# Second norm, merge, tail and the order of an expert step in a hybrid decoder step

## The reference

```python
z = x @ w_in                                  # RWKV, windowed attention, memory attention, 3 gates
o_a, o_b, o_m = rwkv(z), window_attention(z), memory_attention(z)
g = sigmoid(gates)                            # three blocks of 1024
merged = g[0] * (o_a @ p_a) + g[1] * (o_b @ p_b) + g[2] * (o_m @ p_m)
x = LayerNorm(ALPHA * x + merged @ w_o) * ln1_g + ln1_b
# top 1 of 4 groups, top 2 of its 8 experts, blocks of rows per expert
for e in range(32):
    y[e] = (silu(rows[e] @ e_gate[e]) * (rows[e] @ e_up[e])) @ e_down[e]
x = LayerNorm(ALPHA * x + sum_k gate_k * y_k) * ln2_g + ln2_b
```

## Time and profile before

| what | value |
|---|---|
| median of 3 runs | 1317.51 us (1314.8 to 1317.7) |
| the profiled execution | 1323.6 us, of which 1321.8 us lie between its first and its last instruction |
| TensorE busy, mean granted clock | 86%, 0.958 |
| VectorE, ScalarE, GpSimd busy | 33%, 18%, 7% |
| HBM read and written | 277.11 MB, 24.23 MB |
| expert loads (page, DMA issues) | 32 gate, 32 up, 2048 KB each, 36.9 us from issue to landing |
| DMA of GpSimd's queue | 5184 packets, 8.54 MB |

### The profile page before, as it was taken

The page is one execution under the profiler, slowest core; times in us unless marked ns, Lnnn a source line. Parts: engine busy times, 40 slices in busy tenths (PEclk is TensorE's granted clock), DMA queues, the critical chain, the costliest instruction groups (busy, mean ns, idle before and its releaser), DMA issues.

```text
span 1321.8 us, 21992 instructions
## 1 busy us (share of the span) xinstructions
PE 1133.8 (86%) x9315; PEld 792.9 (60%) x9315; DVE 432.0 (33%) x824; ACT 238.1 (18%) x413; POOL 98.7 (7%) x92
## 2 busy tenths in 40 slices
PE   7999989999899999999899944999877777777775
PEld 4888866777678888877774533455444444444432
DVE  5200003576555676524342245111111111111116
ACT  4000011234621111121110110121111111111102
POOL 0400000000000000000001100111111111111110
PEclk9999998899999999999999955999999999999998
DMA  9342242312221101242638064999999999999974
GB/s 332 124 137 64 79 143 63 89 49 72 56 53 56 50 27 46 64 157 75 244 110 336 32 282 178 387 420 425 421 422 425 422 423 424 424 423 422 423 295 194
DMA packets 53346, 293.04 MB, mean 222 GB/s; under 512 B 9995, under 2 KB 12109, under 8 KB 41738
## 3 DMA queue, kind: packets, MB, share of 16 engines
q1 hardware_dynamic: 48098, 283.55, 55.3%
q0 software_dynamic: 5184, 8.54, 1.7%
HBM read 277.11 MB, written 24.23 MB: 228 GB/s over the span
## 4 chain that ended last, share of the span: by engine, by line
PE 60%; DMA 25%; DVE 5%; SPq 4%; ACT 2%; issue 2%; DVEq 1%; POOL 0%; POOLq 0%; ACTq 0%
PE psum L717 57%; DMA arena<-in_e_down 19%; DVE arena L1536 3%; SPq L673 3%; PE psum L722 3%; DMA arena<-in_e_up 3%; ACT arena L1291 1%; DMA arena<-scratch_x,arena 1%; DMA arena<-in_p_abm 1%; DVE arena L1539 1%; DVEq L1571 0%; DMA arena<-in_w_mem_kv 0%; DMA arena<-in_w_in 0%; DMA arena<-scratch_ya 0%; SPq L661 0%
## 5 line engine op out<-in xcount | busy, mean ns | idle before, releaser
L717 PE MATMUL psum<-arena 64*64 64x64 f32 (+9 forms) x8808 | 1068.4, 337 | 151.9 <-DMA arena<-in_e_gate 31.8
L717 PEld LDWEIGHTS psum<-arena 64*64 64x64 f32 (+3 forms) x8808 | 738.5, 152 | 459.4 <-issue 218.8
L1291 ACT ACTIVATE arena<-psum 128x512 f32<-128x512 f32 (+11 forms) x144 | 88.1, 635 | 657.1 <-PE psum L717 393.6
L1536 DVE TENSOR_TENSOR arena<-arena,psum 128x256 f32<-128x256 f32 (+3 forms) x136 | 74.6, 548 | 342.5 <-PE psum L717 202.7
L1536 DVE TENSOR_TENSOR arena<-arena 128x1024 f32<-128x1024 f32 (+16 forms) x173 | 133.7, 784 | 33.5 <-PE psum L717 8.7
L722 PE MATMUL psum<-arena 128*128 128x128 f32 (+5 forms) x507 | 74.8, 281 | 22.1 <-DMA arena<-scratch_x,arena 8.1
L722 PEld LDWEIGHTS psum<-arena 128*128 128x128 f32 (+5 forms) x507 | 54.8, 145 | 54.6 <-issue 32.1
L1536 DVE TENSOR_TENSOR arena<-psum,arena 128x256 f32<-128x256 f32 (+4 forms) x85 | 47.0, 564 | 68.6 <-PE psum L717 64.4
L2186 POOL TENSOR_TENSOR arena<-arena 128x1024 f32<-128x1024 f32 (+1 forms) x10 | 27.2, 2733 | 469.0 <-DVE arena L1536 469.0
L2127 DVE COPY arena<-arena 128x1 uint32 (+1 forms) x32 | 4.9, 154 | 153.9 <-PE psum L717 153.9
L2231 POOL DMA_INDIRECT arena<-scratch_x,arena x32 | 32.7, 1023 | 283.0 <-DVE arena L2118 242.0
(11 more groups left out here) (114 smaller groups left out, 200.1 us busy)
## 6 DMA issues: line engine op xcount, KB each, us to landing
arena<-in_e_gate SPq DMA_DIRECT2D x32, 2048.0 KB, 36.9
arena<-in_e_up SPq DMA_DIRECT2D x32, 2048.0 KB, 36.9
arena<-in_e_down SPq DMA_DIRECT2D x21, 2048.0 KB, 36.8
arena<-in_w_in SPq DMA_DIRECT2D x46, 512.0 KB, 3.9
arena<-in_e_down SPq DMA_DIRECT2D x44, 512.0 KB, 34.4
scratch_gates<-arena SPq DMA_DIRECT2D x24, 260.0 KB, 4.1
arena<-scratch_gates SPq DMA_DIRECT2D x8, 780.0 KB, 4.5
arena<-in_p_abm SPq DMA_DIRECT2D x8, 640.0 KB, 5.7
```

Source lines behind the costliest of these rows:

```text
L717: return pe.matmul(out, a, b, start=start, stop=stop)
L1291: return act.activation(out, a, ACT.Copy)
L1536: return v.tensor_tensor(out, a, b, op)
```

## The change

- Merge: the window and memory projections of block 1 move from ahead of the group norm's spreading to behind branch 0 of block 0, and VectorE's products with them.
- Second norm: the transposes take the scaled row, ahead of gain and bias (`turn_normed`), and gain and bias come in at the eviction as a scalar per partition from a new tile `lnT` (one more small load on SyncE's queue), half of the channels on ScalarE, half on VectorE. The transposes of a tile stand between the halves of the next tile's `w_o` product, the logits behind it. Gain and bias of the rows themselves are both VectorE's, GpSimd's `offset(x1, 1)` is gone.
- Routing: the comparison rounds become a rounding by addition and subtraction of 1.5 * 2^23.
- Expert stage: down(e-1) stands ahead of up(e), on TensorE and in SyncE's queue. The last down matrix comes in two loads, and its product waits for each half apart.
- Tail: no lag; each tile is finished on VectorE with two passes of 1024 (subtract the mean and multiply by the gain; multiply by the reciprocal and add the bias); ScalarE makes only the root. GpSimd reads its register ahead of the last scatter's wait.

```diff
+HALF_DOWN = 0.5 / SB - 0.5
+WHOLE = 1.5 * 2.0 ** 23
...
@@ SyncE @@
             sp.dma_start(gb[:, 1, :], I["ln1_b"].partition_broadcast(P)).then_inc(s["out_in"], 16)
+            sp.dma_start(lnT, I["ln1_T"]).then_inc(s["out_in"], 16)
...
                     gate_load(e, (j - 1) % 3, e - 3)
+                    down_load(e - 1, (j - 2) % 3, e - 4)
                     up_load(e, j % 3)
-                    down_load(e - 1, (j - 2) % 3, e - 4)
-            down_load(NE - 1, (NE - 2) % 3, NE - 4)
+            sp.wait_ge(s["y_mm"], NE - 1)
+            sp.dma_start(ed[0][:, 0:2, :], wd[NE - 1][:, 0:2, :]).then_inc(s["ew0d_in"], 16)
+            sp.dma_start(ed[0][:, 2:4, :], wd[NE - 1][:, 2:4, :]).then_inc(s["out_in"], 16)
...
@@ TensorE @@
             gate_tile(G_MERGE + 1, (G_MERGE + 1) % 2, (G_MERGE + 1) // 2, 6)
-            pe.wait_ge(s["mgw1_in"], 32)
-            for g in (1, 2):
-                pe.wait_ge(s["proj_used"], g)
-                project(1, g, 2 * (g - 1))
...
-            pe.wait_ge(s["proj_used"], 3)
+            pe.wait_ge(s["proj_used"], 1)
             gate_tile(G_MERGE + 2, (G_MERGE + 2) % 2, (G_MERGE + 2) // 2, 0)
             pe.wait_ge(s["oa_ready"], 1)
-            for q in range(2):
-                project(q, 0, 4 + 2 * q)
+            project(0, 0, 4)
+            pe.wait_ge(s["mgw1_in"], 32)
+            pe.wait_ge(s["proj_used"], 2)
+            project(1, 1, 2)
+            pe.wait_ge(s["gate_out"], G_MERGE + 3)
+            project(1, 2, 0)
+            project(1, 0, 6)
...
+            def turn_normed(step):
+                u = tile_at(1, step)
+                n = rows(u)
+                pe.wait_ge(s["ln_scaled"], step + 1)
+                if step:
+                    pe.wait_ge(s["x1T_ready"], 2 * step)
+                for c in range(KD):
+                    last = turn(bank(4, KD, P)[:, c, 0:n], x1[0:n, u, c::KD])
+                last.then_inc(s["x1_turned"], 1)
...
+            for step in range(1, Q):
+                t = tile_at(1, step)
+                if step >= 2:
+                    pe.wait_ge(s["h_used"], step - 1)
+                for h in range(2):
                     for c in range(KD):
-                        last = turn(bank(4, KD, P)[:, c, 0:n], x1[0:n, u, c::KD])
-                    last.then_inc(s["x1_turned"], 1)
-                if step >= 2:
-                    logits(step - 2)
+                        last = mm(bank(2 * (step % 2) + h, 512), MG[:, c, t * P:t * P + P], wo[h][:, c, :], c == 0, c == KD - 1)
+                    if h == 0:
+                        turn_normed(step - 1)
+                last.then_inc(s["h_made"], 1)
+                logits(step - 1)
+            turn_normed(Q - 1)
             logits(Q - 1).then_inc(s["logits_made"], 1)
...
                 for k in range(FF // P):
+                    if half_in and k == 2:
+                        pe.wait_ge(s["out_in"], half_in)
...
                 turn_h_step(e - 1)
+                down_step(e - 1, d % 3, i * 2 + d // 3)
                 up_step(u % 3, i * 2 + u // 3)
                 if not last:
                     rows_step(e + 1, (j + 1) % 2, i * 3 + (j + 1) // 2)
-                down_step(e - 1, d % 3, i * 2 + d // 3)
...
-            down_step(NE - 1, (NE - 2) % 3, (NE - 2) // 3)
+            down_step(NE - 1, 0, (NE - 2) // 3, 112)
...
@@ ScalarE @@
-                copy(x1T[:, :, t * P:t * P + n], bank(4, KD, P)[:, :, 0:n]).then_inc(s["x1T_ready"], 1)
-
-            layer_norm(x1, 1, 0, before=lambda t: x1_turned(t - 1) if t >= 1 else None)
-            x1_turned(Q - 1)
+                for c in range(KD // 2, KD):
+                    last = act.activation(x1T[:, c, t * P:t * P + n], bank(4, KD, P)[:, c, 0:n], ACT.Identity,
+                                          bias=lnT[:, 1, c:c + 1], scale=lnT[:, 0, c:c + 1])
+                last.then_inc(s["x1T_ready"], 1)
+
+            act.wait_ge(s["out_in"], 96)
+            layer_norm(x1, 1, 0, after=x1_turned)
...
-            layer_norm(x1, 2, 1, tail=True)
+            for u in range(Q):
+                t = tile_at(2, u)
+                n = rows(t)
+                act.wait_ge(s["ln_stats"], 2 * Q + u + 1)
+                act.activation(rstd[0:n, t, :], mv[0:n, t, 1:2], ACT.Sqrt, bias=eps[0:n, 0:1]).then_inc(s["ln_std"], 1)
...
@@ VectorE @@
-            attention_branches(1)
...
+            v.wait_ge(s["gate_sig"], 2)
+            for n, (g, b) in enumerate(((1, 2), (2, 0), (0, 6))):
+                v.wait_ge(s["proj_made"], 4 + n)
+                gated(1, 1, g, b, n == 0)
+            v.sem_inc(s["merged"], 1)
...
-                        tt(x[0:n, i, :], x[0:n, i, :], gb[0:n, 0, :], ALU.mult).then_inc(s["ln_gained"], 1)
-                        if tail:
-                            v.drain()
-                            tt(x[0:n, i, :], x[0:n, i, :], gb[0:n, 1, :], ALU.add).then_inc(s["x_normed"], 1)
+                        if turned:
+                            turned(i, u)
+                        tt(x[0:n, i, :], x[0:n, i, :], gb[0:n, 0, :], ALU.mult)
+                        v.drain()
+                        tt(x[0:n, i, :], x[0:n, i, :], gb[0:n, 1, :], ALU.add).then_inc(s["x_normed"], 1)
...
-            ts(qb, rank, float(SB), ALU.is_ge)
-            ts(nx, cnt, float(SB), ALU.is_gt)
-            v.drain()
-            for q in range(2, N // SB + 1):
-                stt(qb, rank, float(SB * q), qb, ALU.is_ge, ALU.add)
-                stt(nx, cnt, float(SB * q), nx, ALU.is_gt, ALU.add)
-                v.drain()
+            ts(qb, rank, 1.0 / SB, ALU.mult, HALF_DOWN, ALU.add)
+            ts(nx, cnt, 1.0 / SB, ALU.mult, HALF_DOWN - 1.0 / SB, ALU.add)
+            v.drain()
+            ts(qb, qb, WHOLE, ALU.add)
+            ts(nx, nx, WHOLE, ALU.add)
+            v.drain()
+            ts(qb, qb, WHOLE, ALU.subtract)
+            ts(nx, nx, WHOLE, ALU.subtract, 0.0, ALU.max)
+            v.drain()
...
-            layer_norm(x1, 2, expert_sum, 1, tail=True)
+            for u in range(Q):
+                t = tile_at(2, u)
+                n = rows(t)
+                expert_sum(t, u)
+                src = bank(2 * t, D) if t < NT else x1[0:B, NT, :]
+                for h in range(2):
+                    v.bn_stats(st6[0:n, t, h, :], src[:, h * 512:(h + 1) * 512])
+                v.drain()
+                v.bn_aggr(mv[0:n, t, :], st6[0:n, t, :, :]).then_inc(s["ln_stats"], 1)
+                v.drain()
+                stt(x1[0:n, t, :], src, mv[0:n, t, 0:1], gb[0:n, 0, :], ALU.subtract, ALU.mult)
+                v.wait_ge(s["ln_std"], 2 * Q + u + 1)
+                v.reciprocal(rstd[0:n, t, :], rstd[0:n, t, :])
+                v.drain()
+                stt(x1[0:n, t, :], x1[0:n, t, :], rstd[0:n, t, :], gb[0:n, 1, :], ALU.mult, ALU.add).then_inc(s["x_normed"], 1)
...
@@ GpSimd @@
-            offset(x1, 1)
...
             scatter(NE - 2, 0)
+            n_extra = extra_count(g)
             scatter(NE - 1, 1)
```

More of the change, by code:

```diff
@@ L431, in tile_at, with extra_count, extra_blocks @@
             return (t - 1) % Q if pas else t
[L433 to L435 removed]
+        def extra_count(eng):
+            return eng.value_load(ovfi.bitcast(I32)[0:1, XB:XB + 1], min_val=0, max_val=XB)
+        def extra_blocks(eng, body, n=None):
+            n = extra_count(eng) if n is None else n
             with eng.If(n > 0):
@@ new lines, in turn_normed @@
+            def turn_normed(step):
[7 more added lines that the diff above has]
+                last.then_inc(s["x1_turned"], 1)
+            pe.wait_ge(s["gate_out"], N_GATE)
+            for c in range(KD):
+                for h in range(2):
+                    last = mm(bank(0, 512)[h * 64:h * 64 + B, :], MG[:, c, T:N], wo[h][:, c, :], c == 0, c == KD - 1)
@@ L1293, in _, with layer_norm @@
             eps = const("eps")
-            def layer_norm(x, pas, lag, before=None, after=None, tail=False):
+            def layer_norm(x, pas, lag, before=None, after=None):
                 scaled = s["x_scaled" if pas == 0 else "ln_scaled"]
@@ L1307, in layer_norm @@
                         act.wait_ge(s["ln_rs"], pas * Q + u + 1)
-                        src = bank(2 * i, D) if tail and i < NT else x[0:n, i, :]
+                        src = x[0:n, i, :]
                         act.activation(x[0:n, i, :], src, ACT.Identity, bias=nmr[0:n, i, :],
@@ L1544, in ts, with layer_norm @@
                 return v.tensor_scalar(out, a, s1, s2, op0, op1)
-            def layer_norm(x, pas, before, lag, tail=False):
+            def layer_norm(x, pas, before, lag, turned=None):
                 for t in range(Q + 2 * lag):
@@ L1967, in residual, with x1_turned @@
                 v.drain()
-            layer_norm(x1, 1, residual, 0)
+            def x1_turned(t, at):
+                n = rows(t)
+                v.wait_ge(s["x1_turned"], at + 1)
+                for c in range(KD // 2):
```

(5 more changed lines are left out.)

68 lines of the change are left out of this document (23 added, 45 removed).

## The result

| what | before | after |
|---|---|---|
| median | 1317.7 us (9 runs) | 1309.3 us (9 runs, 1304.6 to 1312.9) |
| ratio, 95% interval | | 0.9934 [0.9915, 0.9953], so 8.7 us less, between 6.2 and 11.2 |
| profiled execution: span | 1321.8 us | 1307.1 us |

The profiled executions differ by 14.7 us, more than the medians, since 5.1 of these lie ahead of the merge, in code that the change leaves alone: the eviction of the gate tile that the merge waits for stands at 605.73 before and at 600.65 after. The clock differs by as much: up to that eviction TensorE lost 17.1 us to the lower level in the one execution and 12.0 in the other. The sections on the experiments and on the hardware tell more of such differences. From here on only lengths of stretches are compared, each from an event that both kernels have.

What follows compares the result with a forecast made beforehand. The prediction took the DMA engines to bound the expert stage, with chains of waits before and behind it. Its terms, 5.7 + 2.45 + 2.44 - 2.0 - 0.45 + 0.5 + 3.2 = 11.8, took 1317.5 to 1305.7 us, range 1300 to 1311.

Steps and rivals of the forecast that it cites:

- Merge: Merge: waits for loads of 4.26 and 0.48 us and 1.7 of clock go, 0.75 is added; gain 5.7, bounds 3.0 to 7.2.
- Second norm: Last tile's chain: 3.70 and 1.6 us saved, 2.85 added ahead; gain 2.45, bounds 1.5 to 5.0.
- Routing: Routing on VectorE: three of eight pairs of comparisons are left; five fewer save 2.44 us.
- Expert stage: Expert stage, DMA-bound: the new order costs 2.0 us in the first steps and 0.45 at the end.
- Tail: Scatter to reload gains 0.5 us; third norm gains 3.2, the sample tile's passes moving into waits, 4.3 per prompt tile.
- The later third pair: First expert steps: up(1)'s load goes out 4.6 us later and the DMA engines run dry, losing 2.2 to 3.7 us.
- the old dip: First expert steps: the DMA share's dip to 0.78 at 848 to 852 us goes, giving back 0.9 us.
- The term for GpSimd's read: Scatter to reload: the register read is done earlier, under the last scatter's wait; gain 0.5 us, bounds 0 and 1.1.
- The first: Rival, expert stage: short idles bring cold spells and TensorE becomes the bound; about 1361 us, slower; chance 3%.
- one of the prediction's own signs of being wrong: Expert stage: a granted clock below 1.00 in its middle would show the prediction wrong.
- The second: Rival: DMA engines run dry longer in the expert stage (-4.6) and merge gives only 3.0; 1311 us; chance 17%.
- The third: Rival: clock stays up through the shorter waits of norm and spreading, +2.6 and +1.5; 1301.6 us; chance 15%.

Runs made afterwards that it cites:

- after_again: The kernel after, unchanged, run once more for a second trace: 99.1 us from the first w_o product to the scan.
- tail_only: The kernel before with only the third norm's change and GpSimd's early read: 29.6 us from the first product of the residual to VectorE's end.

## Why the prediction was right, and where it was not

The time, 1309.3, lies in the range and 3.6 us above the forecast of 1305.7. Part of that is luck: second norm and routing gave 2.4 us less than forecast and the merge 1.1 less, but the expert stage took 1.6 less than forecast. By stretches, means over all traces that have the old or the new form:

| stretch | old | new | gained | forecast |
|---|---|---|---|---|
| merge: gate tile's eviction to first w_o product | 86.9 | 82.3 | 4.6 | 5.7 |
| second norm and routing: to the scan | 101.2 | 98.7 | 2.5 | 4.9 |
| scan to the issue of eu2 | 20.7 | 20.7 | 0 | 0 |
| expert stage: to the first product of the residual | 469.9 | 470.7 | -0.9 | -2.45 |
| tail: to VectorE's end | 33.6 | 30.2 | 3.4 | 3.7 |
| sum | | | 9.6 | 11.8 |

**Second norm, the step that failed.** In the first pair of traces the norm itself took 85.2 us before and 85.9 after, and routing the rest: the term came out at -0.7 instead of +2.45. The prediction worked out the last tile's chain, and that came as it said. It set the first tile's at nothing and did not follow ScalarE's side of it: two waits ahead of a first square root, a table load behind the later one, and transposes moved to where they need the result. 1.43 us of wait and 1.7 of clock are the 3.1 missing. In the four traces with the early table load the term is 2.1 to 2.8, 2.4 on the mean, which is the forecast. The Trainium skill, "ScalarE: Activation LUTs", section on what ACT_TABLE_LOAD costs, measures about 1283 ns for the load and 1380 for a drain; the row agrees on the load (1.28), and the drain does not show. It does not show either where the load stands straight between an eviction and the next function (in the trace of after the eviction ends at 601.25, the load stands at 601.27 to 602.55, the function follows at 602.56).

**Merge.** The removed wait, its hiding and the new 0.79 were right. Mis-sized was what the clock gives back: 1.7 was taken for the spell behind the wait, with the other one kept at 1.5. The spell behind the spreading is not a constant: where it lost 1.7 the stretch gained just 5.7 (86.9 - 81.2), where 3.4, about 4.0. Why it is 1.7 in one execution and 3.4 or 5.1 in another is not shown.

**Routing.** 2.9 us (16.0 before, 13.1 after, from the last logits to the scan) against 2.44: the three rounds left have one tensor operand and take 0.24 per 128x160 instruction where those removed took 0.33, which makes it 2.7 by the rounds (3.91 - 1.23). The other 0.24 lies ahead of them, where VectorE had stood 0.46 us in the trace of before and does not in that of after; that is not explained.

**Expert stage.** The later third pair (4.9 us, 4.6 worked out) and a dip were right, and the dip is smaller: shares 0.85 and 0.82 over 8 us, 1.3 us, not 2.2 to 3.7. In its first window TensorE is busy 4.00 of 4.00 us: there the loads wait for TensorE. That the old dip goes in return rested on the earlier trace rows, and that was one execution's. At the end of the stage 0.9 of the stream's loss of 1.4 is left. The prediction let the end cost 0.45 more; in the first trace of after the chain leads through the landing of x1 instead of the last scatter, but where the rest goes was not tried and stays open.

**Tail.** 4.3 us per tile and the sum were right. The term for GpSimd's read was too small, 0.5, and the prediction found no row for it, but the traces have one. The chain of the kernel before, and below it that of after_again (the last scatter, then the reload):

```profile
1287.42 0.49 POOLq L435
```

```profile
1274.36 4.09 DMA scratch_ya<-arena
1278.75 2.71 DMA arena<-scratch_ya
```

The read took 0.49 us, less than the least that the prediction cites for it. From the landing of the last scatter to the reload it is 1.10 us before (1287.33 to 1288.43) and in the three other traces without the early read, and 0.30 in all ten with it (1278.45 to 1278.75 here): 0.8 saved. How much of it reaches the end is open, since in tail_only and in the first trace of after the chain runs through the landing of x1 instead.

**Rivals.** The first did not come as it stood: from 60 to 420 us behind eu2 the DMA share is 0.99 or more in every window of 10 us, in all traces. But a weak form of it came, and with it one of the prediction's own signs of being wrong, a granted clock below 1.00 in the middle of the stage. Each of the six traces with the new order has one or two cold spells of 1.7 us, 240 to 290 us behind eu2, and none of the eight with the old order has one there. The first trace of after (timeline and window), and the longest wait at this place in the first trace of before:

```profile
1042.69 5.36 PE L724 MATMUL psum<-arena 128*64 128x256 f32 x32 [2.12 <-DMA arena<-in_e_up]
1044.00:1048.00 4.00, 4.00 (x25) 2.08 (x21) 0.00 (x0) 0.00 (x0) 0.00 (x0) 0.60 0.99 422
```

```profile
1091.88 3.68 PE L717 MATMUL psum<-arena 128*64 128x256 f32 x32 [1.70 <-DMA arena<-in_e_gate]
```

TensorE's longest wait in this part of the stage is 2.1 to 2.5 us with the new order and 1.7 with the old, and every spell stands at a wait of 1.9 to 2.5 us for an up load, though not every such wait has one. Nothing of what the spells cost shows in the DMA share. So the rule of the Trainium skill, "TensorE: Matmul & The Clock Gate", section on a second failure mode, is borne out here in small part: with short idles in every step the clock fell in one or two of some 28 steps, and by the waits at these places it was the longer idles that went with it.

The second gave nearly the right time, 1311, from other causes than its own: the merge's lower end came in some executions, a longer dry time of the DMA engines in none. The third came nowhere in full: the clock fell ahead of the last logits in all nine traces with the new norm, and the merge kept at least one spell in all ten with the new merge.

## What to carry to other kernels

When an edit puts a second wait ahead of an engine's first use of a function, look where the table load now stands, and whether the consumer that used to come later has been moved up to it; a wait is best put at the one instruction that needs it. When a change makes a chain shorter, follow the first item through it as well as the last. Before a dip or a spell is put into a sum, ask whether it is the program's or that execution's: a second trace of the same kernel answers it.

## What the runs showed of the hardware

Losses to the clock came in whole portions. Over fourteen traces the stretch of the merge lost 1.7, 3.4 or 5.1 us, the second norm up to its last w_o products 0 or 1.7, and the unchanged part ahead of the merge 8.5 to 17.1, in steps of 1.7. The stretch from the first w_o product to the scan, on the other hand, was 101.2 in all five traces of the old norm. Two executions of before differ by 8.5 us of clock ahead of the merge (17.1 and 8.5 lost, the eviction at 605.7 and 598.7), about as much as their spans, 1321.8 and 1313.9. In the three executions of after it is 12.0 each, and they differ by the portions in merge and norm (1307.1, 1308.8 and 1304.8). So much of the spread of this kernel's times is that, and a change of 2 us is seen in stretches, not in single times.
